# A hybrid conformer trunk step: the norms' sample products stand in PSUM strips instead of in SBUF

## The reference, cut to what matters

```
x = x + HALF * gt1 * _swiglu(_rmsnorm(x, g_ffn1) * (1 + sc1) + sh1, w_ffn1_up, w_ffn1_down)
hm = _rmsnorm(x, g_mix) * (1 + scm) + shm
proj = hm @ w_in
...
x = x + gtm * mix
x = x + HALF * gt2 * _swiglu(_rmsnorm(x, g_ffn2) * (1 + sc2) + sh2, w_ffn2_up, w_ffn2_down)
```

## Time and profile before

| | us |
|---|---|
| median of 3 timed runs | 1062.1 |
| lowest, highest | 1060.46, 1062.18 |
| the profiled execution, its own time | 1052.43 |
| its span in the profile | 1050.6 |

### The profile page before, as it was taken

How to read it: one execution, slowest core, us unless ns; L and a number is a source line. 1 busy time by engine, 2 the same in 40 slices (tenths; PEclk the granted TensorE clock), 3 DMA queues, 4 the chain that set the end, 5 groups by cost and what they waited for, 6 DMA issues and landing times.

```text
span 1050.6 us, 19674 instructions
## 1 busy us (share of the span) xinstructions
PE 1020.2 (97%) x7798; PEld 978.4 (93%) x7798; DVE 604.8 (58%) x1082; ACT 447.4 (43%) x731; POOL 487.7 (46%) x328
## 2 busy tenths in 40 slices
PE   8799999999999999989999998999999999999996
PEld 7699999999999999979976897999999999999996
DVE  2796532565433664669989436975335674246464
ACT  4555421355312553353343524655314554135532
POOL 2246443455533555535872033456444655345641
PEclk8999999999999999989999998999999999999998
DMA  8642365132361232425244422132322232313222
GB/s 318 232 188 81 127 252 223 41 118 85 121 240 41 84 118 90 150 98 223 82 100 173 161 80 81 41 121 81 121 81 81 81 101 101 119 43 110 92 80 90
DMA packets 21685, 127.46 MB, mean 121 GB/s; under 512 B 4192, under 2 KB 5344, under 8 KB 7008
## 3 DMA queue, kind: packets, MB, share of 16 engines
q1 hardware_dynamic: 15456, 96.06, 25.4%
q10 hardware_dynamic: 6144, 30.19, 7.7%
HBM read 123.06 MB, written 3.19 MB: 120 GB/s over the span
## 4 chain that ended last, share of the span: by engine, by line
PE 90%; DVE 6%; ACT 2%; POOL 1%; issue 1%; DVEq 0%; ACTq 0%; POOLq 0%
PE tile_a L457 20%; PE tile_b L457 20%; PE tile_b L511 15%; PE tile_a L511 15%; PE ada_ps L511 12%; PE tile_a L699 2%; PE ada_ps L429 2%; DVE sq L1276 1%; PE tile_a L631 1%; DVE sq L1273 1%; PE stat_ps L569 1%; POOL x_lo L1675 1%; ACT x_hi L904 1%; PE stat_ps L577 1%; DVE x_lo L1260 0%
## 5 line engine op out<-in xcount | busy, mean ns | idle before, releaser
L1689 POOL TENSOR_TENSOR w_lo<-w_raw,w_hi 128x512 fp32r<-128x512 f32 x120 | 159.2, 1327 | 219.6 <-ACT w_hi L817 218.0
L1653 POOL TENSOR_TENSOR w_lo<-w_raw,w_hi 128x2048 fp32r<-128x2048 f32 x29 | 133.4, 4599 | 195.3 <-ACT w_hi L790 195.3
L1689 POOL TENSOR_TENSOR w_lo<-s_raw,w_hi 128x512 fp32r<-128x512 f32 x80 | 103.0, 1310 | 24.4 <-ACT w_hi L817 24.4
L817 ACT ACTIVATE w_hi<-w_raw 128x512 fp32r<-128x512 f32 x120 | 75.8, 632 | 69.8 <-PE tile_b L457 18.6
L790 ACT ACTIVATE w_hi<-w_raw 128x2048 fp32r<-128x2048 f32 x32 | 61.1, 1911 | 84.4 <-PE tile_b L457 81.9
L817 ACT ACTIVATE w_hi<-stat_ps 128x512 fp32r<-128x512 f32 x80 | 47.5, 596 | 84.4 <-DVE s_raw L1358 80.8
L457 PE MATMUL tile_a<-h_hi,w_hi 128*128 128x288 f32 x352 | 75.5, 296 | 0.0
L457 PE MATMUL tile_b<-h_hi,w_hi 128*128 128x288 f32 x352 | 75.0, 295 | 0.0
L457 PE MATMUL tile_a<-h_hi,w_lo 128*128 128x288 f32 x352 | 74.9, 294 | 0.0
L457 PE MATMUL tile_b<-h_hi,w_lo 128*128 128x288 f32 x352 | 74.9, 294 | 0.0
L457 PE MATMUL tile_b<-h_lo,w_hi 128*128 128x288 f32 x352 | 74.8, 294 | 0.0
(11 more groups left out here) (215 smaller groups left out, 2579.4 us busy)
## 6 DMA issues: line engine op xcount, KB each, us to landing
w_raw<-w_units SPq DMA_DIRECT2D x78, 1024.0 KB, 4.8
ada_raw<-w_ada ACTq DMA_DIRECT2D x28, 1024.0 KB, 6.7
ada_raw<-w_ada SPq DMA_DIRECT2D x8, 1024.0 KB, 5.2
x<-x_in SPq DMA_DIRECT2D x4, 576.0 KB, 5.9
y_out<-x SPq DMA_DIRECT2D x8, 288.0 KB, 2.4
conv_s<-conv_state SPq DMA_DIRECT2D x1, 480.0 KB, 5.9
conv_s_out<-conv_s ACTq DMA_DIRECT2D x1, 480.0 KB, 4.2
wp_raw<-w_pool SPq DMA_DIRECT2D x1, 256.0 KB, 5.7
```

The costliest lines, as they stand in the source:

```text
L817: nc.scalar.activation(slot(w_hi, i), source, ACT.Copy).then_inc(ready, 1)
L1653: nc.gpsimd.tensor_tensor(w_lo[:, side, :], w_raw[:, side, :], w_hi[:, side, :].bitcast(F32), ALU.subtract).then_inc(w_lo_ready, 1)
L1689: return nc.gpsimd.tensor_tensor(slot(w_lo, i), raw, slot(w_hi, i).bitcast(F32), ALU.subtract)
```

## The change

The two sample strips of 64 columns leave `sq` and stand in bank 1 of `stat_ps`, even chunks at columns 128 to 191 and odd chunks at 192 to 255, past the 64 columns that 1/rms takes there. L1255 writes its product there, L1276 multiplies it there in place, and L1283 reads it there. The prompt's part stays in `sq`. No instruction is added, removed or moved, and no semaphore or wait changes.

```
+        def sample_ps(c):
+            first = TOKENS - 512 + DEC_SEQ * DEC_BATCH * (1 + c % 2)
+            return stat_ps[:, 1, first:first + DEC_SEQ * DEC_BATCH].rearrange("p (h n) -> p h n", h=2)
...
-                    nc.vector.tensor_tensor(sample(by_half(sq[:, c % 2, :])), sample(by_half(x[:, c, :])), sample(r),
+                    nc.vector.tensor_tensor(sample_ps(c), sample(by_half(x[:, c, :])), sample(r),
                                             ALU.mult).then_inc(norm_s1, 1)
...
-                    nc.vector.tensor_tensor(steps(sample(t)), steps(sample(t)), over_steps(gain[:, n, c, 1:ROWS]),
+                    nc.vector.tensor_tensor(steps(sample_ps(c)), steps(sample_ps(c)), over_steps(gain[:, n, c, 1:ROWS]),
                                             ALU.mult).then_inc(norm_s2, 1)
...
-                    nc.vector.tensor_tensor(steps(sample(f)), steps(sample(t)),
+                    nc.vector.tensor_tensor(steps(sample(f)), steps(sample_ps(c)),
                                             over_steps(mod[:, SHIFT[n], c, 1:ROWS]), ALU.add).then_inc(norm_fs, 1)
```

## The result

The changed kernel took 1051.68 us (median of 6 runs, 1049.96 to 1053.47), the kernel before 1061.48 in the same measurement (6 runs, 1060.46 to 1062.3). The changed kernel's profiled execution, one of the six, took 1049.96 (span 1048.2), only 2.5 less than the 1052.43 of the one before. Its lines stand four further down: L1255, L1276, L1283, L1260, L1675 and L1662 are L1259, L1280, L1287, L1264, L1679 and L1666.

A forecast was written before the change was run, and what follows sets the result against it. TensorE, busy 97% of the span, was taken as the bound, its largest wait being for VectorE's L1260. Norm gains 1.4 + 1.8 + 1.8 = 5.0 us took 1062.1 to 1057.1, range 1053.0 to 1060.8.

The forecast's parts named there:

- the remaining 1.0 to 1.3: Second norm, up to the next unit: us of TensorE waiting for chunks and L1662; taken as 1.25 gained.
- the 0.69 and 0.4 of the third: Third norm: 0.69 us of waiting for L1675 at the end and 0.4 between chunks would go.
- rival C: L1276 and L1283 still read one SBUF tensor and stay held, so nothing moves: 1062; chance 0.08.
- The operations' own cost: The 72 moved VectorE operations take 224 ns each, 1.0 us in all, priced at 0; upper bound 282 ns.
- rival D: PSUM results come late between L1255, L1276 and L1283, making it slower: 1067 at 0.30 us late; chance 0.05.
- First norm: Last chunk's hold of L1276 goes, partly moving to L1260; TensorE restarts earlier: gain 1.4 us (1.0 to 1.7).
- Rival B: GpSimd's hold moves to L1260, directly in front of TensorE: gain only 2.4 us, 1059.7; chance 0.13.
- Second norm: TensorE begins sooner and no longer waits for chunks: gain 1.8 us (1.4 to 2.0).
- The term for the start: Second norm: without the first L1276's hold, TensorE begins near 457.75 instead of 458.32, 0.55 us sooner.
- Rival A: Shorter waits in the norms also reduce low-clock time, 3.2 us more: 1053.9; chance 0.20, wholly or partly.
- Third norm: TensorE starts 1.3 us sooner and waits at the end and between chunks go: gain 1.8 us (1.7 to 2.3).
- What passes on: Behind each norm, later work and the wait for L852 move with it, so the gains sum to 5.0 us.

The follow-up runs named there:

- repeat: The changed kernel, unedited, measured and profiled a second time beside the kernel before: 1055.85 us, ratio 0.9937.
- filler: Extra transposes into unused PSUM in TensorE's waits for the three norms, in both kernels: before 1061.37 us, changed 1054.61 us.
- 96 columns: The changed kernel with four extra matmuls of 96 columns in the whole run: 1056.59 us, ratio 0.994.
- four of 48: Four extra matmuls of 48 columns in the whole run, added to each kernel: before 1055.25 us, changed 1049.84 us.
- many of 48: 31 extra matmuls of 48 columns added to each kernel: before 1058.26 us, changed 1052.05 us.

## Why the prediction was wrong

**The step that failed** is "The timed median, 1062.1, is 9.7 above that execution; I take the same 5.0 from it". It took the 9.7 for a constant of the measurement. It was a second time of the same kernel: about 8 us of it were the matmuls' quick pace in the second feed-forward part, as the second trace of before showed. A change that shifts TensorE's stream can change how often that pace comes up, and the range had no term for it. The changed kernel's repeat, 1055.85, is inside the range; the first measurement, 1051.68, is not.

Over five comparisons (repeat, filler, 96 columns, four of 48, many of 48) the change gives 5.3 to 6.8 us by the medians, against the 5.0 forecast; the first measurement's 9.7 lies some 3 to 4 above that. Two things can make these 3 to 4 us, and their shares stay open. One is the pace: the one trace of the changed kernel there had the quick one for 320 us. Of the 103 runs of the kernel before beside these experiments three lie at 1052.6 to 1053.0, at ordinary clocks (0.981 to 0.985), as its first trace, and none between them and 1059.6; so timed runs can have it too. The other is the clock: the five other timed runs of the changed kernel had a mean granted clock of 0.986 or 0.987, its profiled one 0.981, and eight of the nine in the repeat 0.980 to 0.985 (of the first measurement's runs of before the clock isn't on record). Runs of the kernel before at 0.984 are 2.5 us shorter in the median than those at 0.980 (24 and 14 runs), so 0.003 of clock is worth some 2 us, an estimate. There is no trace of a timed run, so none of this is shown for them.

**A term that was too small** is what waiting for chunks cost behind TensorE's restart, "the remaining 1.0 to 1.3" of the second norm and the 0.69 and 0.4 of the third. In the first pair of traces it gave 1.9 and 1.7. The three norms together were 7.4 us shorter there (1.5, 3.5 and 2.4) and not 5.0; 1.9 of it was given back in the mixer's stage, where the changed kernel's trace has a clock of 0.57 from 581 to 585 us, and 3.0 behind the third norm, which leaves the 2.4 between the two spans.

**The mechanism** was right. L1276 was held by GpSimd and is not with an input in PSUM (721 to 226 ns); one free input is enough, which the kernel with only the first product in PSUM shows from the other side. That excludes rival C. The Trainium skill (SBUF — State Buffer, Who interferes with whom) says that an operation of VectorE with at most one SBUF input doesn't contend with GpSimd. All 72 operations agree with it: in the first trace the longest of L1259 and L1280 took 0.230 us, of L1287 0.226.

**The operations' own cost**: forecast 224 ns each, measured 226, 221 and 224. No latency between them through PSUM shows in the pair's 2.93 us, so rival D is out. The page's larger overhead on PSUM (Perfetto Trace Analysis, Optimizing Scalar/DVE Operations; the Trainium skill again) isn't borne out by these three rows.

**First norm**: forecast 1.4, TensorE's restart at 50.3 and the hidden product at 53.0; measured 50.61 and 53.13 in the first trace. In seven traces with the change the hidden product comes at 51.8 to 53.1, in eight without it at 53.1 to 55.2; by the run with this norm alone the gain is 2.0 (0.3 to 3.6). Right within that scatter; L1264 took 1.17 where some 1.4 was expected. Rival B's hold came here, as forecast, and elsewhere only in a few first chunks, by up to 0.25 (0.96 in the second norm of the first trace).

**Second norm**: forecast 1.8; measured 3.3 to 3.9 in six traces, 2.0 in a seventh, and 2.2 (1.1 to 3.3) timed. The term for the start was too small. In both traces of before the first L1276 ends just behind L1662, 4.3 us behind the reciprocal, and TensorE restarts at 6.4; only how early 1/rms arrives differs, and with it how long L1276 is held. The 0.91 in the earlier trace rows was one outcome, the second trace has 1.60:

```profile
454.46 2.37 POOL L1662 TENSOR_TENSOR w_lo<-w_raw,w_hi 128x1024 fp32r<-128x1024 f32 x1 [7.44 <-ACT w_hi L790]
...
455.31 1.60 DVE L1276 TENSOR_TENSOR sq<-sq,gain 128x64 f32<-128x64 f32 x1
```

After the change the restart came at 5.0 to 5.9, 0.6 to 1.5 sooner (1.46 in the first trace) and not 0.55. The second term is the stretch from the restart to the next unit. It was priced as 15.3 us of TensorE's work out of 16.3, but in eight traces without the change in this norm the next unit starts 22.7 us behind the reciprocal, with anything from 0 to 5.3 us of low clock in the work: the chunks, and GpSimd's L1662 behind them, set it. In the changed kernel's first trace L1666 is done 1.06 before TensorE gets there, without a wait, and the stretch is 14.35 us:

```profile
466.26 2.39 POOL L1666 TENSOR_TENSOR w_lo<-w_raw,w_hi 128x1024 fp32r<-128x1024 f32 x1
...
469.71 0.50 PE L461 MATMUL tile_a<-x_hi,w_hi 128*128 128x288 f32 x2
```

Rival A isn't what made the gain here: with no low clock behind the restart the norm took 19.1 to 19.4 us (three traces), with 3.0 to 3.4 us of it 19.4 to 19.6 (three more); the seventh had 4.4 and took 20.9.

**Third norm**: forecast 1.8; the pair of chunks was forecast well (2.95 against 2.93), and the norm is 2.0 to 4.1 us shorter in seven traces. TensorE's restart, forecast 1.3 sooner, was 0.7 sooner in the first trace (5.7 behind the reciprocal against 6.4). Before, the norm takes 22.7 us in eight traces, with 0 to 4.5 us of low clock in the work; after, 18.6 and 19.5 with none, 19.25 to 20.75 with 2.8 to 6.0. So once the chunks come faster the clock does count here, and rival A is true in part. In five of the seven traces the clock was low at the first fast unit behind the norm, and 0.8 to 1.4 was given back (2.1 in the first trace, whose low stretch at the last norm also begins earlier, at 1035). Two traces without the change in this norm have such a stretch too, so where it falls isn't set by this change alone; it was in no term.

**What passes on** held: between the norms the lead stays what it was to within 0.1 us in the table, the wait for L856 moved with the norm ahead of it. It didn't shrink, though: 4.1 us in two waits before, 4.7 after, in the second traces.

## What to carry to other kernels

When the profiled execution and the timed median of a kernel lie nearly 1% apart, find out first what differs, by a second profile of the same kernel; a forecast from one trace is otherwise tied to whichever of two times the trace has. On VectorE an operation with both inputs in SBUF beside a busy GpSimd was held for up to GpSimd's whole operation (2.29 us); one input in PSUM frees it for some 10 ns, but the next such operation takes the hold over, so the whole chain has to be looked at. A low clock in a stretch that another engine paced cost nothing here: raise it in the kernel before (here by filler) and see whether the stretch gets shorter, before it is priced. To compare two kernels whose time has such a second pace, break the stream at fixed places in both: the scatter of before fell to 2.1 us with many extra matmuls, that of the changed kernel only to 5.9.

## What the runs showed of the hardware that was not expected

TensorE's stream of 288-column matmuls has two paces at a granted clock of 1.00, 0.1300 and 0.1333 us each. Either one goes on for up to 320 us until an irregularity, and a single extra matmul of 48 columns, which costs about 0.1 us, turned common into quick in 49 of 51 cases over the five traces that have it, and quick into common in 28 of 28. The Trainium skill (TensorE: Matmul & The Clock Gate, Part 1) gives the spacing of back-to-back matmuls at 2.4 GHz as the columns' time and some 2.5 ns; by that estimate it would be 0.1225 us here. No stretch reached it; here each matmul has a weight load of its own (7798 of both in the first trace of before). With four such matmuls the changed kernel is the quickest here: 1049.84 in the median, 1040.29 at best, ratio 0.9882 (0.9855 to 0.9909). Open is why the widths sort the pace as they do, and why the timed runs with four of them take the quick pace less often than the profiled ones. That wasn't tried further.
